# A trunk of feed-forward and mixer layers on one Trainium2 core: the feed-forward layers in two stages, with the high part of a weight tile meeting both parts of x in one 512-column pass

## The reference

```python
D_FF = ((8 * D_MODEL // 3 + 127) // 128) * 128      # 2816

def _swiglu(h, w_gate, w_up, w_down):
    return (jax.nn.silu(h @ w_gate) * (h @ w_up)) @ w_down

for i in range(DEPTH):
    x = x + 0.5 * _swiglu(_rms_norm(x, norm_ffn1[i]), ffn1_w_gate[i], ffn1_w_up[i], ffn1_w_down[i])
    h = _rms_norm(x, norm_mix[i])
    ...                                             # y: fox, conv, diff or fox mixer of h
    x = x + y
    x = x + 0.5 * _swiglu(_rms_norm(x, norm_ffn2[i]), ffn2_w_gate[i], ffn2_w_up[i], ffn2_w_down[i])
```

## Time and profile before

| | |
|---|---|
| runs | 2136.3, 2137.06 and 2136.75 us |
| the profiled execution: its span on the core | 2137.5 us; the page gives no other time of it |
| PE busy | 2076.1 us, 97% of the span, 16546 matmuls |
| DVE busy | 1377.3 us, 64% |
| ACT busy | 960.1 us, 45% |
| POOL busy | 124.8 us, 6% |
| from memory | 341.38 MB, 160 GB/s over the span |
| chain that ended last | PE 86%, DVE 9%, issue 2%, ACT 2% |

### The profile page before, as it was taken

One profiled execution on the slowest core, in us unless ns is written; L12 is line 12 of the kernel. 1 busy time (PEld: TensorE's weight loads), 2 busy tenths in 40 slices (PEclk: granted clock), 3 DMA queues, 4 the chain that ended last, 5 costly groups with the idle time before them and its releaser, 6 DMA issues.

```text
span 2137.5 us, 39342 instructions
## 1 busy us (share of the span) xinstructions
PE 2076.1 (97%) x16546; PEld 2001.7 (94%) x16546; DVE 1377.3 (64%) x1532; ACT 960.1 (45%) x1057; POOL 124.8 (6%) x119
## 2 busy tenths in 40 slices
PE   7999999999999998899999999999999999999999
PEld 7999788999999997799999998799999999889999
DVE  6655767655755689565575558875557556776555
ACT  4435556334433440543453345564435435455442
POOL 2000301000200003100010000010001001101000
PEclk9999999999999999899999999999999999999999
DMA  6655333655455550165555554345555555434552
GB/s 198 198 184 178 119 118 119 197 184 189 150 186 186 167 178 8 59 208 179 178 177 192 182 175 139 118 138 182 190 178 178 180 191 161 122 117 159 189 184 98
DMA packets 261367, 343.73 MB, mean 161 GB/s; under 512 B 8086, under 2 KB 233887, under 8 KB 261279
## 3 DMA queue, kind: packets, MB, share of 16 engines
q1 hardware_dynamic: 261134, 342.41, 49.4%
q10 hardware_dynamic: 144, 0.05, 0.0%
HBM read 341.38 MB, written 1.05 MB: 160 GB/s over the span
## 4 chain that ended last, share of the span: by engine, by line
PE 86%; DVE 9%; issue 2%; ACT 2%; DMA 0%; DVEq 0%; POOL 0%; ACTq 0%; POOLq 0%
PE bank L1295 27%; PE bank L1297 26%; PE bank L1296 26%; DVE sb_w_low L735 3%; DVE sb_x_low L771 2%; PE bank L1427 2%; DVE sb_x_square L1182 2%; PE bank L1475 1%; DVE sb_xT L762 1%; PE bank L1442 1%; PE bank L1459 1%; PE bank L1430 1%; ACT sb_w_high L442 1%; PE bank L1573 0%; PE bank L1480 0%
## 5 line engine op out<-in xcount | busy, mean ns | idle before, releaser
L735 DVE TENSOR_TENSOR sb_w_low<-sb_raw,sb_w_high 128x2048 fp32r<-128x2048 f32 x324 | 757.1, 2337 | 449.9 <-ACT sb_w_high L442 448.9
L1295 PE MATMUL bank<-sb_x_high,sb_w_high 128*128 128x256 f32 x3328 | 950.9, 286 | 20.4 <-DVE sb_w_low L735 20.4
L1297 PE MATMUL bank<-sb_x_high,sb_w_low 128*128 128x256 f32 x3328 | 944.7, 284 | 0.0
L1296 PE MATMUL bank<-sb_x_low,sb_w_high 128*128 128x256 f32 x3328 | 944.4, 284 | 0.0
L442 ACT ACTIVATE sb_w_high<-sb_raw 128x2048 fp32r<-128x2048 f32 x324 | 616.7, 1904 | 178.5 <-PE bank L1297 178.4
L1295 PEld LDWEIGHTS bank<-sb_x_high,sb_w_high 128*128 128x128 f32 x3328 | 641.5, 193 | 27.9 <-DVE sb_w_low L735 24.1
L1296 PEld LDWEIGHTS bank<-sb_x_low,sb_w_high 128*128 128x128 f32 x3328 | 641.1, 193 | 1.5 <-issue 1.4
L1297 PEld LDWEIGHTS bank<-sb_x_high,sb_w_low 128*128 128x128 f32 x3328 | 640.9, 193 | 0.0
L1295 PE MATMUL bank<-sb_h_high,sb_w_high 128*128 128x256 f32 x1408 | 394.4, 280 | 0.0
L1296 PE MATMUL bank<-sb_h_low,sb_w_high 128*128 128x256 f32 x1408 | 392.8, 279 | 0.0
L1297 PE MATMUL bank<-sb_h_high,sb_w_low 128*128 128x256 f32 x1408 | 392.8, 279 | 0.0
(11 more groups left out here) (198 smaller groups left out, 1722.2 us busy)
## 6 DMA issues: line engine op xcount, KB each, us to landing
sb_raw<-in_ffn_w_gate SPq DMA_DIRECT2D x88, 1024.0 KB, 5.3
sb_raw<-in_ffn_w_up SPq DMA_DIRECT2D x88, 1024.0 KB, 5.3
sb_raw<-in_ffn_w_down SPq DMA_DIRECT2D x88, 1024.0 KB, 4.8
sb_raw<-in_fox_w_in SPq DMA_DIRECT2D x24, 1024.0 KB, 5.3
sb_raw<-in_conv_w_pw SPq DMA_DIRECT2D x12, 1024.0 KB, 5.4
sb_raw<-in_diff_w_in SPq DMA_DIRECT2D x12, 1024.0 KB, 5.0
sb_raw<-in_fox_w_out SPq DMA_DIRECT2D x8, 1024.0 KB, 4.8
sb_raw<-in_diff_w_out SPq DMA_DIRECT2D x4, 1024.0 KB, 4.8
```

The costliest lines, as they stand in the source:

```text
L735: dve.tensor_tensor(w_low[b % RING][:, :], raw[b % RING][:, :], w_high[b % RING][:, :].bitcast(F32), ALU.subtract).then_inc(S["low_ready"], 1)
L1295: pe.matmul(dst, s_high, m_high, start=first, stop=False, skip_group_check=loose)
L1296: pe.matmul(dst, s_high, m_low, start=False, stop=False, skip_group_check=loose)
L1297: return pe.matmul(dst, s_low, m_high, start=False, stop=last, skip_group_check=loose)
```

## The change

The three passes of a triple become two in the FFNs. `x_both` holds high and low part of a tile of x side by side, 512 columns, and `both_parts` streams them in one pass through the high part of the weights: columns 0 to 255 of a bank collect high by high, columns 256 to 511 high by low. The low part of the weights meets the high part of x in a second pass of 256 columns, added to the upper columns. So one output tile of 128 features fills a whole bank in two halves that have to be added. ACT copies the upper halves out (`upper_half`, `gate_part`, `up_part`) and DVE adds the lower ones (`gate`, `up`): for each pair two more ACT and two more DVE operations. A pair now takes four banks, and pairs alternate between banks 0 to 3 and 4 to 7.

The FFN has two stages. All 11 pairs come first, and `h_both` keeps the split hidden features of all of them. Then the down projection runs by output tiles: for T = 0 to 3 two output tiles of 128 features are summed over all 22 hidden tiles, from three blocks (`DOWN`: 8, 8 and 6 tiles, 256 columns wide) in banks 0 and 1 or 2 and 3. When T is finished, x of these tiles is updated with two DVE operations, and split, while PE works on T + 1; only T = 3 remains for the boundary (`begun`). The first pair of an FFN goes through gate and up together, two tiles of x at a time (`first_pair`), then PE sums the squares into bank 3 and waits for the root before pair 1.

The ring has five slots. The low part is written over `raw` in place, so that a block is loaded when PE has finished the block five before it, and ACT no longer waits for PE. Blocks b and b + 1 of a phase are split before its boundary. Hardware loops over weight blocks are unrolled. Scratch of the mixers shares memory with `h_both`; POOL therefore clears the padding of the convolution at the start of that phase (`pads_ready`). The output is turned and stored in four parts, three of them between the last down blocks. The mixers keep `three_passes`.

```diff
-RING = 3
+RING = 5
+FF_TILES = D_FF // P
+DOWN = [(0, 8), (8, 16), (16, FF_TILES)]
...
+        with ExitStack() as landing:
+            raw = landing.enter_context(nc.sbuf_tensor("sb_raw", [P, RING, 2048], F32))
+        w_low = sb("w_low", [P, RING, 2048], F32R)
+        w_high = sb("w_high", [P, RING, 2048], F32R)
...
-                    sp.wait_ge(S["low_ready"], b - RING + 1 + u * per)
-                dst = raw[b % RING][:, :].rearrange("p (k n) -> p k n", k=src.shape[1])
+            def load(b, src):
+                if b >= RING:
+                    sp.wait_ge(S["block_done"], b - RING + 1)
...
+                    for p in range(PAIRS):
+                        load(b + 2 * p, columns(wg, 256 * p))
...
+                    for T in range(4):
+                        for c, (first, last) in enumerate(DOWN):
+                            load(b + 2 * PAIRS + len(DOWN) * T + c,
+                                 wd[first * P:last * P, 256 * T:256 * T + 256].rearrange("(k p) n -> p k n", p=P))
...
+                act.wait_ge(raw_landed[b % RING], 16 * (b // RING + 1))
+                act.activation(slot(w_high, b)[:, 0:width(b)], slot(raw, b)[:, 0:width(b)], ACT.Copy
+                               ).then_inc(S["high_ready"], 1)
...
                     act.wait_ge(S["norm_copied"], 1)
-                    for T in range(4):
-                        high(T)
                     split_high(0)
-                    for T in range(4):
-                        square(T)
                     split_high(1)
-                else:
-                    split_high(starts[i] + 1)
-                    for T in range(4):
-                        high(T)
-                        square(T)
+                for T in range(3 if i and phases[i - 1] == "ffn" else 0, 4):
+                    high_and_square(i, T)
                 width = SEQ + 2 if phases[i] in ("fox", "diff") else SEQ
                 act.wait_ge(S["sumsq_done"], i + 1)
...
+                def upper_half(p, which):
+                    at = pair_banks(p) + 2 * which
+                    act.wait_ge(S["block_done"], b + 2 * p + which + 1)
+                    act.activation((up_part if which else gate_part)[:, :, :], banks[:, at:at + 2, SEQ:], ACT.Copy
+                                   ).then_inc(S["up_part_ready" if which else "gate_part_ready"], 1)
...
+                for p in range(PAIRS):
+                    split_high(b + 2 * p + 3)
+                    upper_half(p, 0)
+                    silu(p)
+                    split_high(b + 2 * p + 4)
+                    upper_half(p, 1)
+                    high(p)
+                e = b + 2 * PAIRS
...
+                elif phases[i - 1] == "ffn":
+                    sums = banks[:, out_banks(T), :]
+                    dve.scalar_tensor_tensor(xT[:, 2 * T:2 * T + 2, :], sums[:, :, SEQ:], 0.5,
+                                             xT[:, 2 * T:2 * T + 2, :], ALU.mult, ALU.add).then_inc(S["x_half"], 1)
+                    dve.wait_ge(S["x_half"], 4 * sum(k == "ffn" for k in phases[:i - 1]) + T + 1)
+                    dve.scalar_tensor_tensor(xT[:, 2 * T:2 * T + 2, :], sums[:, :, 0:SEQ], 0.5,
+                                             xT[:, 2 * T:2 * T + 2, :], ALU.mult, ALU.add).then_inc(S["x_ready"], 1)
...
+                begun = 3 if i and phases[i - 1] == "ffn" else 0
+                for T in range(begun, 4):
                     update_x(i, T)
-                    if T:
-                        low(T - 1)
...
+                def gate(p):
+                    at = pair_banks(p)
+                    c = PAIRS * f + p + 1
+                    dve.wait_ge(S["gate_part_ready"], c)
+                    dve.tensor_tensor(gate_part[:, :, :], banks[:, at:at + 2, 0:SEQ], gate_part[:, :, :],
+                                      ALU.add).then_inc(S["gate_sum_ready"], 1)
+                    dve.wait_ge(S["gate_sum_ready"], c)
+                    dve.tensor_tensor(pair(gate_in[:, :]), gate_part[:, :, :], over_tokens(inv_rms[:, 0:SEQ]),
                                       ALU.mult).then_inc(S["gate_in_ready"], 1)
...
+                for p in range(PAIRS):
+                    gate(p)
+                    split_low(b + 2 * p + 3)
+                    scaled(p)
+                    up(p)
+                    split_low(b + 2 * p + 4)
+                    low(p)
+                e = b + 2 * PAIRS
...
-                if last:
-                    one_pair(PAIRS - 2)
-                    one_pair(PAIRS - 1)
+                for T in range(3):
+                    for k in range(3):
+                        split_low(e + 3 * T + 3 + k)
+                    update_x(i + 1, T)
...
+            def both_parts(at, n, high, low, m_both, first, last):
+                def on_low():
+                    pe.matmul(bank[at][:, SEQ:2 * SEQ], low[:, n * P:(n + 1) * P], m_both[:, 0, :],
+                              start=False, stop=False, skip_group_check=True)
+                if not first:
+                    on_low()
+                ins = pe.matmul(pair(bank[at][:, :]), high[:, n * P:(n + 1) * P], m_both[:, :, :],
+                                start=first, stop=last, skip_group_check=True)
+                if first:
+                    on_low()
+                return ins
             def columns_half(dst, b, n):
...
+                def tile(which, p, n, ks):
+                    blk = b + 2 * p + which
+                    high, low = (slot(t, blk).rearrange("p (k n) -> p k n", k=KT) for t in (w_high, w_low))
+                    for k in ks:
+                        ins = both_parts(pair_banks(p) + 2 * which + n, n, high[:, k, :], low[:, k, :],
+                                         x_both[:, k, :, :], k == 0, k == KT - 1)
+                    return ins
+                def first_pair():
+                    wait_block(b)
+                    wait_block(b + 1)
+                    if f:
+                        pe.wait_ge(S["hidden_ready"], PAIRS * f)
+                    for T in range(4):
+                        pe.wait_ge(S["xlow_ready"], 8 * i + 2 * T + 2)
+                        for which in range(2):
+                            for n in range(2):
+                                ins = tile(which, 0, n, (2 * T, 2 * T + 1))
+                            if T == 3:
+                                ins.then_inc(S["block_done"], 1)
+                def one_pair(p):
+                    pe.wait_ge(S["hidden_ready"], PAIRS * f + p - 1)
+                    for which in range(2):
+                        wait_block(b + 2 * p + which)
+                        for n in range(2):
+                            ins = tile(which, p, n, range(KT))
+                        ins.then_inc(S["block_done"], 1)
+                def down(T, c):
+                    blk = b + 2 * PAIRS + len(DOWN) * T + c
+                    first, last = DOWN[c]
+                    wait_block(blk)
+                    if T == 0:
+                        pe.wait_ge(S["h_low_ready"], PAIRS * f + last // 2)
+                    elif c == 0 and T >= 2:
+                        pe.wait_ge(S["x_ready"], 4 * (i + 1) + T - 1)
...
+                    for n in range(2):
+                        for t in range(first, last):
+                            ins = both_parts(2 * (T % 2) + n, n, high[:, t - first, :], low[:, t - first, :],
+                                             h_both[:, t, :, :], t == 0, t == FF_TILES - 1)
+                    ins.then_inc(S["block_done"], 1)
...
+                sum_squares(i, 3)
+                pe.wait_ge(S["root_ready"], i + 1)
+                for p in range(1, PAIRS):
+                    one_pair(p)
+                for T in range(4):
+                    for c in range(len(DOWN)):
```

471 lines of the change are left out of this document (222 added, 249 removed).

## The result

The changed kernel takes 2143.5 us (median of six runs, 2141.6 to 2146.3), the kernel before on the same chip 2136.5: ratio 1.0032, 95% interval 1.0021 to 1.0044. It is slower by a third of a per cent, where I had forecast 2072 us and 3% faster. The profiled execution has a span of 2144.1 us, 6.6 more than before. Of the six runs three had a mean granted clock of 0.981 or 0.982 and took 2144.5 to 2146.3 us, the profiled one among them, and three had 0.985 and took 2141.6 to 2142.5.

The account below looks back on a forecast made before the run. PE's passes were taken to bound the kernel. Terms of -98.4 + 28 + 13.6 - 5.3 - 5.4 - 2 + 4.3 + 1.3 = -64 took the span from 2137.5 to 2073.6; forecast median 2072 us, range 2052 to 2122.

Parts of the forecast that it names:

- The passes: PE in the FFNs: a 512-column pass replaces two of 256 and takes 0.215 us, -98 us for eight FFNs.
- rival B: PE's passes: reading bounds them, a 512-column pass takes as long as the two it replaces; 2170 us, chance 0.08.
- A: PE's passes: a fixed cost per pass, so a long pass takes 0.226 us; 2118 us, chance 0.11.
- The wait behind the sum: After each FFN's sum of squares PE waits for block b + 2's split, 5.05 us instead of 1.57; +28 us.
- The clock: After each of eight sums the clock drops to half speed for 3.4 us; +14 us, bounds 0 and 27.
- Pair stage, DMA: Gate and up pairs and block loads: DVE and ACT keep up, loads arrive in time; 0 us each.
- C: Pair stage: DVE's round grows by 2 us and leads, 80 pairs cost 1 us each; 2152 us, chance 0.04.
- Phase 3: FFN 5.3 us longer than its sisters: the split delayed by POOL's diagonals now lies ahead of the boundary; -5.3 us.
- The first fox mixer: ACT's tables and a split ahead of the first x now lie under the last down tile; -5.4 us.
- the convolution and diff: The other three mixers: a split of 2.3 us leaves their start; -2 us, between 0 and -7.
- the first FFN: DVE's small table work now stands before the down weights of T = 1; estimated +3 us, between 0 and twice that.
- The start: First FFN starts later, two blocks and both high parts going ahead of most of x; estimated +1.3 us.

Follow-up runs that it names:

- the filled gap: Changed kernel with 36 more passes of 256 columns, result unread, behind each sum of squares: 2129.2 us, 0.9964 of the kernel before.
- the early split: Changed kernel with both splits of block b + 2 moved ahead of the root and reciprocal in each FFN: 2098.3 us, 0.9821 of the kernel before.

## Where the prediction went wrong

The rows from which an FFN is measured, from one sum to the next: before, changed, with the filled gap, with the early split.

```profile
904.08 0.59 PE L1349 MATMUL bank<-sb_square_sum,sb_ones 128*128 128x256 f32 x2
...
1094.91 0.38 PE L1349 MATMUL bank<-sb_square_sum,sb_ones 128*128 128x256 f32 x1
```

```profile
1100.33 0.59 PE L1368 MATMUL banks<-sb_square_sum,sb_ones 128*128 128x256 f32 x2
```

```profile
1089.99 0.38 PE L1368 MATMUL banks<-sb_square_sum,sb_ones 128*128 128x256 f32 x1
```

```profile
1077.67 0.59 PE L1370 MATMUL banks<-sb_square_sum,sb_ones 128*128 128x256 f32 x2
```

Phase 5 lasts 190.83, 193.56, 190.73 and 186.92 us. I had forecast 183.7 for the second.

- **The passes: this step failed.** Predicted -98 us; the long pass was put at 0.215, "nearest in length" to the float32 passes of the convolution. It costs 0.232 to 0.236. The filled kernel has the wait of the changed one and no slow clock, and equals the kernel before: its passes must save what its wait adds, 3.7 us an FFN, **-30 us** in all, and this agrees with 0.010 x 352 = 3.5 from the starts. (The 0.1177 that I used for a down pass isn't what the earlier trace rows give, 0.1166; the starts in the trace are 0.118 apart, so nothing hangs on it.) All of it lies in gate and up; a merged down triple takes the 0.353 of the kernel before, and more than the 0.339 that the same order of work takes unmerged. The long pass is over the 0.231 from which I had said that rival B decides. B is what happened in kind, columns and not a fixed cost set the pass, though it expected no saving at all (0.240 and 2170 us); the time lies between A and B.
- **Why the working misled.** I read that a load starts with the pass before it and that the next pass starts when the load can be through the earlier trace rows, and concluded that the load is the only bound. It is one, at 0.106 to 0.114 for 128 columns, but another lies just above it: four-byte columns go at about 0.46 ns, and 256 of them take 0.113 to 0.120. Two bounds so close can't be told apart in a kernel with one size of pass. The passes of the convolution are four-byte too, but take two cycles a column, so the rate of reading doesn't show in them: right in length, wrong in kind. The transposes had it no better.
- **The wait behind the sum: right.** 5.05 expected, 5.23 measured, with ACT's and DVE's operations in the order given: +29 us against +28. What I left unasked is why the split should stand there: both engines had idled for 7 us ahead of it.
- **The clock: right in kind, a little small in size.** One interval of 3.4 us per sum was expected, +14; there are one or two, 44 us in all, and the filled gap prices them at some 17 us in the FFNs between the two profiled executions (15 between the medians, with all else that differs). The bound of 27 held.
- **Pair stage, DMA: right.** No wait for a hidden tile or a bank, no transfer on the path; C did not happen.
- **Phase 3: right.** From sum to sum it is 186.8 us, as phase 6, where before it had 195.4 against 190.9: its 5 us are gone. The first fox mixer gave back 4.1 of 5.4, the convolution and diff 1.2 and 1.4. In the first FFN +3 was forecast for DVE's small tables, and it is 3.3 longer than the others: a wait of 1.92 us with a slow interval after it. The start was forecast at +1.3 and came out at -1.8, so that sign was wrong, and no run asked why.

Per section, with the 5.7 us that the first pair is longer than the first block taken out: five FFNs in ordinary places are 1.3 to 2.7 us longer, 2.0 in the mean, 15.7 for eight (+29 + 17 - 30 = 16; the 17 and the 30 are differences to the same filled kernel, so of this sum only the 0.010 us a triple, read from the starts, is an independent check); first FFN +3.3 beyond that, phase 3 -4.9, mixers -6.6, start -1.8, end +0.9: together +6.6, the difference between the spans.

**What stays open.** Whether the 0.46 ns are the reading from memory or the handling of this type inside PE: no kernel here mixed two-byte weights with four-byte columns. Why the pair with loads of 128 columns shows as a longer long pass is open too. Why down passes of 256 columns run at 0.113 in one kernel and at 0.118 in another, so that merging them costs time there, and gate and up at 0.120 unmerged but 0.350 a triple merged, was not found.

## What to carry to other kernels

When passes are to be made longer, look for the cost of a longer pass of the same type; rows of another type don't give it, and if none exists, a size sweep in one kernel costs one run. When a step of preparation stands behind a reduction that everybody waits for, ask which of it depends on the reduction at all: here one moved split took 45 us off, where 4224 passes fewer had brought 30. A gap on PE is paid a second time in the clock; 36 useless passes in each gap bought back some 15 us.
